# Gate halves ahead of the transposes in one branch, turned probabilities ahead of chunk splits in another

## The chip, the cores and the metric

The kernel runs on one core of one Trainium2 chip. The metric is the device time of one execution in microseconds; lower is better. TensorE is called PE here, VectorE DVE, ScalarE ACT, GpSimd POOL and SyncE SP, as in the profile.

## The reference, cut to what matters

Two layers of a streaming encoder run for 512 prompt frames and 8 running streams of 16 frames. Each layer mixes three attention branches and then applies a feed-forward part:

```python
h = _rms(x, p['norm_mix'])
(fq, fk, fv, fg, bq, bk, bv, iq, ik, iw, cqa, ckva, ckpe) = jnp.split(h @ p['w_in'], ...)
ya = fox attention(fq, fk, fv, decay)              # branch 1, "fox", 6 heads
yb = attention over the keys an indexer picks      # branch 3, "dsa", 4 heads
yc = latent attention with a rotary part           # branch 2, "mla", 6 heads
g = jax.nn.sigmoid((h @ p['w_gate']))              # gates: 1024 -> 3072
ga, gb, gc = jnp.split(g, 3, axis=-1)
x = x + (ga * ya @ ... + gb * yb @ ... + gc * yc @ ...) @ p['w_o']
x = x + SwiGLU(_rms(x))
```

The indexer of branch 3 scores all keys with 8 heads and keeps the best ones for each frame; 128 of them for the prompt.

## The kernel before, in words

**Items and steps.** The attention of a layer is cut into 88 items, in this order: 24 prompt items of the first branch (fox, one head and one tile of 128 queries each), 8 stream items of it (foxs, steps from `I_FOXS` = 24), 24 prompt items of the second branch (mla, steps from `I_MLA` = 32), 8 stream items (mlas, from `I_MLAS` = 56), 16 of the third branch (dsa, from 64) and 8 of its streams. A prompt item of query tile t has 128(t+1) keys, so its tiles are 128, 256, 384 or 512 columns wide; t goes 0, 0, 1, 1, 2, 2, 3, 3 over eight mla items. Every engine runs through the same steps, in its own order. An item goes through a softmax pipeline: PE computes `scores(i)` at step i, DVE the negated row maximum (`maxima`), ACT the exponential (`exp`), DVE the reciprocal of its sum, ACT multiplies by it at step i+1 (`normalise`), PE transposes the probabilities at step i+2 (`turn`), ACT copies them from PSUM (`turned_out`), and PE multiplies them with the values at step i+3 (`values`; for prompt items once for four items). The scores of item i use PSUM bank i % 3. The transposes use bank 3, or bank 7 where the side work leaves it free.

**Side work.** `SIDE[step]` lists other work of a step, sorted by `_ORDER`: indexer heads (`index_split`, `index_turn`, `index`, `index_sum`, steps 0 to 25), the rounds that pick the best keys (`pick`, DVE alone, one in each step from 0), the projections of the second branch (`mla_latent`, `mla_expand`, `mla_norm`, `mla_turn`, around steps 23 to 30), and the keys of its streams (`mlas_keys`, `mlas_norm`, around steps 53 to 61). On PE the first half of a step's list, by number of entries, comes ahead of `turn`, the second half behind `values`; on ACT the whole list comes ahead of `turned_out`.

**Gate halves.** The 48 gate halves are the products of h with `w_gate`: 24 matmuls of 320 columns each (three for each of 8 blocks, since every operand is split into a high and a low part), all into the one PSUM bank 5. PE computes half k in `gate_half(k)` in the step given by `GATE_AT`; it waits until ACT has copied half k-1 out of the bank (`g_moved`). ACT does that copy in `gate_move(k)` in the step after; behind the copy of an odd half it also makes the high part of a weight chunk (`hi`), and DVE the low part (`lo`), which frees the raw chunk for SP's next load. In the second branch's prompt items, the halves 21 to 29 are computed in steps 35, 37, ... 51, half 30 in step 52. In the first branch's prompt items there is one in every even step. `HELD` (half 17, step 22) is new in the change.

**ACT's order in a step** is: `normalise(step-1)`, `outputs(step-4)`, the gate moves of the step before, the side work, `turned_out(step-2)`, `outputs` of stream items, `exp(step)`. In steps that have an `index_turn` (the odd ones from 1 to 23) the gate moves come behind the side work, ahead of `turned_out`. Both are copies with the ACTIVATE instruction of line 1491, told apart by their output: `gst` or `g` is a gate half, `w_hi` a chunk's high part, `probs_t` the turned probabilities, `probs` the normalised ones. Line 945 is a gate half's matmul, 1121 a turn, 1141 the prompt values, 1062 and 1063 the scores of an mla item and their mask, 1205 the last products of `mla_expand`, 1607 the exponential, 1658 the indexer's copy.

Of the kernel before, what the change touches and what calls it, by code (L numbers as in the profile page):

```python
# [59 lines left out]
C_GATE = C_IN + 4 * len(GROUPS)  # L60
# [9 lines left out]
_c, _n = C_FF, C_FF  # L70
# [61 lines left out]
I_FOX, I_MLA, I_DSA = 0, len(FOX_ITEMS), len(FOX_ITEMS) + len(MLA_ITEMS)  # L132
ALL_ITEMS = FOX_ITEMS + MLA_ITEMS + DSA_ITEMS
N_ITEMS = len(ALL_ITEMS)
I_FOXS, I_MLAS, I_DSAS = I_MLA - DECB, I_DSA - DECB, N_ITEMS - DECB
# [9 lines left out]
SIDE = [[] for _ in range(N_ITEMS + 6)]  # L145
# [17 lines left out]
    SIDE[2 * _n].append(("index_split", _n))  # L163
    SIDE[2 * _n + 1].append(("index_turn", _n))
for _n in range(len(PICKS)):
    SIDE[_n].append(("pick", _n))
SIDE[I_DSA + 6].append(("mla_streams", 0))
SIDE[I_MLAS - 10].append(("mla_absorb", 0))
for _k in range(2):
    SIDE[I_MLAS - 13 + _k].append(("mla_rope", _k))  # L170
_ORDER = ("index_sum", "foxs_out", "mlas_out", "dsas_out", "mla_streams", "mla_turn", "mla_rope", "mla_absorb", "mla_norm", "mlas_norm", "mla_expand", "mlas_keys", "mla_latent",
          "foxs", "dsas_keys", "index", "index_turn", "index_split", "pick")
for _side in SIDE:
    _side.sort(key=lambda part: _ORDER.index(part[0]))
# [39 lines left out]
_total, _sum, GATE_AT = sum(GATE_WEIGHT[item[0]] for item in ALL_ITEMS), 0, [-1] * GATE_FIRST  # L214
# [4 lines left out]
                       else _n + (_n == I_MLAS - 3))  # L219
assert len(GATE_AT) == GATE_HALVES  # L220
GATE_KEPT = 6
GATE_LAST, LAST_PARTS = GATE_HALVES - 1, ((0, 3), (3, 6), (6, KD))
GATES_IN = [[_k for _k in range(GATE_HALVES) if GATE_AT[_k] == _n] for _n in range(N_ITEMS + 6)]

# [55 lines left out]
def build_program(nc, io):  # L280
    ctx = ExitStack()
    with ctx:
# [304 lines left out]
        def own_wait(eng, tick):  # L587

            eng.sem_inc(tick.sem, 1)
# [267 lines left out]
        def _(pe):  # L857
# [23 lines left out]
            for L in range(DEPTH):  # L881
# [109 lines left out]
                for c in range(2, C_GATE):  # L991
                    g, k = divmod(c, 4)
# [343 lines left out]
                for step in range(N_ITEMS + 6):  # L1336
                    if step < N_ITEMS:
                        scores(step)

                    half = (len(SIDE[step]) + 1) // 2  # L1340
                    for kind, n in SIDE[step][:half]:
                        beside(kind, n)
                    last_four = step in (I_FOXS + 2, I_MLAS + 2, I_DSAS + 2)
                    if last_four:
                        values(step - 3)
                    if 2 <= step < N_ITEMS + 2:
                        turn(step - 2)
                    if 3 <= step < N_ITEMS + 3 and not last_four:
                        values(step - 3)
                    for kind, n in SIDE[step][half:]:  # L1350
                        beside(kind, n)
                    for k in GATES_IN[step]:
                        if k != GATE_LAST:
                            gate_half(k)
                    if step in (N_ITEMS - 1, N_ITEMS, N_ITEMS + 1):
                        gate_half(GATE_LAST, *LAST_PARTS[step - N_ITEMS + 1])
                    if step == N_ITEMS + 2:
                        pe.wait_ge(it_exp.sem, it_exp.at(L, N_ITEMS))
                        own_wait(pe, pe_tick)
                        pe.wait_ge(lo_made.sem, lo_made.at(L, C_OUTS + 1))  # L1360
                        pe.wait_ge(at_lo.sem, at_lo.at(L, 1))
                        column_tile(0, C_OUTS, 0, 3, (h_hi[:, 0:3, :], h_lo[:, 0:3, :])).then_inc(y_done.sem, 1)
# [126 lines left out]
        def _(act):  # L1489
# [6 lines left out]
            for L in range(DEPTH):  # L1496
# [79 lines left out]
                def gate_move(k):  # L1576

                    m, half = divmod(k, 2)
                    if half:
                        act.wait_ge(w_used.sem, w_used.at(L, C_GATE + m + 1))  # L1580
                    else:
                        act.wait_ge(g_done.sem, g_done.at(L, m + 1))
                    if m >= 3 * GATE_KEPT:
                        dst = graw[m // 3][:, m % 3, half * HALF:(half + 1) * HALF]
                    else:
                        dst = gst[:, half, :]
                        if m:
                            act.wait_ge(g_out[half].sem, g_out[half].at(L, 16 * m))
                    copy(dst, ps[:, 5, 0:HALF]).then_inc(g_moved.sem, 1)
                    if half:  # L1590
                        if k != GATE_LAST:
                            hi(C_GATE + 2 + m, m % 2)

                def heads_out(dst, n, kd, t, h0, scale=1.0):
# [15 lines left out]
                def turned_out(i):  # L1610
                    _, _, _, rows, blocks, _ = item_shape(i)
                    act.wait_ge(it_tr.sem, it_tr.at(L, i + 1))
                    if PT_FREE[i]:
                        act.wait_ge(it_pv.sem, it_pv.at(L, PT_FREE[i]))
                    view = lambda a: a.rearrange("p (j r) -> p j r", r=P)[:, :, 0:rows]
                    copy(view(probs_t[:, PT_AT[i]:PT_END[i]]), view(ps[:, TURN_BANK[i], 0:blocks * P])).then_inc(it_pt.sem, 1)
# [159 lines left out]
                for step in range(N_ITEMS + 6):  # L1776
                    if step == 6:
                        act.wait_ge(store_dsa.sem, store_dsa.at(L, 3 * STORED))
                        act.wait_ge(store_fox.sem, store_fox.at(L, 3 * STORED))
                        act.wait_ge(store_mla.sem, store_mla.at(L, 2 * STORED))  # L1780
                    if 1 <= step <= N_ITEMS:
                        normalise(step - 1)
                    if 4 <= step < N_ITEMS + 4 and item_shape(step - 4)[3] == P:
                        outputs(step - 4)
                    moves = [k for k in GATES_IN[step - 1] if k != GATE_LAST] if step else []
                    turning = any(kind == "index_turn" for kind, n in SIDE[step])
                    if not turning:
                        for k in moves:
                            gate_move(k)
                    if step == N_ITEMS + 2:  # L1790
                        gate_move(GATE_LAST)
                    for kind, n in SIDE[step]:
                        beside(kind, n)
                    if turning:
                        for k in moves:
                            gate_move(k)
                    if 2 <= step < N_ITEMS + 2:
                        turned_out(step - 2)
                    if 3 <= step < N_ITEMS + 3 and item_shape(step - 3)[3] != P:
                        outputs(step - 3)  # L1800
                    if step < N_ITEMS:
                        exp(step)
# [201 lines left out]
        def _(dve):  # L2004
# [9 lines left out]
            for L in range(DEPTH):  # L2014
# [5 lines left out]
                def lo(c, slot, width=1024):  # L2020

                    dve.wait_ge(hi_made.sem, hi_made.at(L, c + 1))
                    high, low = split_of(c)
                    dve.tensor_tensor(low[:, 0:width], raw[raw_slot(c)][:, 0:width], high[:, 0:width].bitcast(F32), ALU.subtract).then_inc(lo_made.sem, 1)  # L2024
# [361 lines left out]
                def at_split(k0, nk, a):  # L2386
                    dve.wait_ge(rows_free.sem, rows_free.at(L, k0 // 3 + 1))
                    dve.wait_ge(tp_out.sem, tp_out.at(L, JOB["mla_streams", 0] + 1))
                    dve.tensor_copy(h_hi[:, k0:k0 + nk, :], a[:, :, :])
                    dve.drain()  # L2390
                    at_rest(k0, nk, a)
# [4 lines left out]
                for it in range(N_ITEMS + 6):  # L2396
                    if it == 0:
                        for k in range(1, GATE_FIRST // 2):
                            lo(C_GATE + 2 + k, k % 2)
                    if it == 6:  # L2400
                        dve.wait_ge(store_dsa.sem, store_dsa.at(L, 3 * STORED))
                        dve.wait_ge(store_fox.sem, store_fox.at(L, 3 * STORED))
                        dve.wait_ge(store_mla.sem, store_mla.at(L, 2 * STORED))
                    if 1 <= it <= N_ITEMS:
                        reciprocal(it - 1)
                    if it < N_ITEMS:
                        maxima(it)
                    if it == N_ITEMS:
                        at_split(0, 3, at_fox)
                    for kind, n in SIDE[it]:  # L2410
                        beside(kind, n)
                    for k in GATES_IN[it - 1] if it else ():
                        if k % 2 and k != GATE_LAST:
                            lo(C_GATE + 2 + k // 2, k // 2 % 2)
                at_split(3, 3, at_mla)
                dve.wait_ge(w_used.sem, w_used.at(L, C_OUTS))
                dve.wait_ge(it_out.sem, it_out.at(L, I_DSAS))
# [94 lines left out]
                for half in range(2):  # L2512
                    k, cols = slice(4 * half, 4 * half + 4), slice(P, T_COPIED * P)
# [211 lines left out]
```

## Time and profile before

| | |
|---|---|
| time, median of 3 runs | 2130.53 us (2129.0 to 2130.67) |
| profiled execution | 2130.57 us, span 2128.8 us |
| PE busy | 2092.0 us (98%) |
| DVE busy | 1394.2 us (65%) |
| ACT busy | 965.3 us (45%) |
| POOL busy | 395.8 us (19%) |
| DMA | 207.84 MB, 98 GB/s on the mean |

Times in the rows below are microseconds from the span's start; "idle before" is the time that the engine had nothing to run just ahead of the instruction, and the arrow names what it waited for. A layer takes about half the span. The steps of the first layer lie at 180 to 261 (fox), 261 to 317 (foxs), 317 to 400 (mla), the same steps of the second layer 1055.5 later.

### The profile page before, as it was taken

How to read it: one execution, taken by the hardware profiler on the slowest of the kernel's cores; microseconds unless marked ns; L12 is line 12 of the kernel's file. 1: busy time of each engine (PE TensorE's matmuls, PEld its weight loads, DVE VectorE, ACT ScalarE, POOL GpSimd, SP SyncE). 2: the span in 40 equal slices, each digit the busy share in tenths (PEclk: the TensorE clock that was granted, in tenths of full speed). 3: DMA queues.
4: the chain of work that ended last, by engine and by line, in shares of the span. 5: the costliest groups of instructions: out<-in, count | busy, mean ns of one | idle time of the engine just before them, and what ended most of it. 6: DMA issues, size and time to landing. Idle time of an engine off the chain costs nothing.

```text
span 2128.8 us, 36960 instructions
## 1 busy us (share of the span) xinstructions
PE 2092.0 (98%) x13616; PEld 1880.5 (88%) x13616; DVE 1394.2 (65%) x2839; ACT 965.3 (45%) x2054; POOL 395.8 (19%) x287
## 2 busy tenths in 40 slices
PE   9999999999999999999999999999999999999999
PEld 8998768788979989989899987787889899899897
DVE  4467876646749838839445778766476597496493
ACT  4246666566335314324232467665663343243241
POOL 1120030200004314224011200203000152241230
PEclk9999999999999999999999999999999999999999
DMA  6233224142422222222232332241424222222222
GB/s 219 76 113 124 72 93 134 56 141 88 139 79 80 88 82 80 86 76 87 78 138 77 111 115 89 80 138 56 150 85 139 80 80 87 73 85 85 80 90 79
DMA packets 90682, 207.84 MB, mean 98 GB/s; under 512 B 20676, under 2 KB 46920, under 8 KB 90184
## 3 DMA queue, kind: packets, MB, share of 16 engines
q1 hardware_dynamic: 90504, 205.48, 28.5%
q8 instruction: 110, 1.80, 0.3%
q14 instruction: 68, 0.56, 0.1%
HBM read 181.50 MB, written 23.95 MB: 97 GB/s over the span
## 4 chain that ended last, share of the span: by engine, by line
PE 91%; DVE 3%; ACT 3%; issue 1%; POOL 1%; DVEq 1%; DMA 0%; SPq 0%; ACTq 0%
PE ps L899 28%; PE ps L945 16%; PE ps L1430 8%; PE ps L1432 8%; PE ps L1431 8%; PE ps L957 7%; PE ps L1121 2%; PE ps L1141 2%; PE ps L1017 2%; PE ps L1062 1%; PE ps L1036 1%; PE ps L1235 1%; PE ps L1410 1%; POOL rsq L1969 1%; DVEq L2017 1%
## 5 line engine op out<-in xcount | busy, mean ns | idle before, releaser
L1491 ACT ACTIVATE w_hi<-raw 128x1024 fp32r<-128x1024 f32 (+4 forms) x172 | 171.2, 998 | 399.5 <-PE ps L899 369.3
L2024 DVE TENSOR_TENSOR w_lo<-raw,w_hi 128x1024 fp32r<-128x1024 f32 (+4 forms) x124 | 139.1, 1123 | 190.2 <-ACT w_hi L1491 186.2
L945 PE MATMUL ps<-h_hi,w_hi 128*128 128x320 f32 x768 | 246.1, 320 | 2.7 <-ACT g L1491 2.7
L945 PE MATMUL ps<-h_hi,w_lo 128*128 128x320 f32 x768 | 237.3, 309 | 0.0
L945 PE MATMUL ps<-h_lo,w_hi 128*128 128x320 f32 x768 | 237.2, 309 | 0.0
L1430 PE MATMUL ps<-th_hi,op_hi 128*128 128x320 f32 x640 | 198.3, 310 | 4.1 <-issue 4.1
L1969 POOL TENSOR_TENSOR rsq<-ssq,mhalf 128x12 f32<-128x12 f32 (+3 forms) x56 | 118.0, 2107 | 443.8 <-DVE ssq L2102 383.9
L1432 PE MATMUL ps<-th_hi,op_lo 128*128 128x320 f32 x640 | 198.5, 310 | 0.0
L1431 PE MATMUL ps<-th_lo,op_hi 128*128 128x320 f32 x640 | 198.2, 310 | 0.0
L899 PE MATMUL ps<-w_hi,act_hi 128*128 128x512 f32 x440 | 174.5, 396 | 0.0
L899 PE MATMUL ps<-w_hi,act_lo 128*128 128x512 f32 x440 | 174.4, 396 | 0.0
L899 PE MATMUL ps<-w_lo,act_hi 128*128 128x512 f32 x440 | 174.4, 396 | 0.0
L1491 ACT ACTIVATE op_hi<-w_sums 128x512 fp32r<-128x512 f32 x160 | 100.1, 631 | 143.5 <-PE ps L1432 117.1
L2485 DVE TENSOR_TENSOR w_lo<-raw,w_hi 128x1024 fp32r<-128x1024 f32 x48 | 59.9, 1252 | 157.9 <-ACT w_hi L1491 157.9
L945 PEld LDWEIGHTS ps<-h_hi,w_hi 128*128 128x128 f32 x768 | 144.3, 188 | 9.1 <-issue 5.9
L1431 PE MATMUL ps<-h_lo,op_hi 128*128 128x320 f32 x480 | 148.6, 310 | 0.0
L1430 PE MATMUL ps<-h_hi,op_hi 128*128 128x320 f32 x480 | 148.4, 309 | 0.0
L1432 PE MATMUL ps<-h_hi,op_lo 128*128 128x320 f32 x480 | 148.3, 309 | 0.0
L899 PE MATMUL ps<-w_hi,h_hi 128*128 128x384 f32 (+3 forms) x440 | 146.4, 333 | 0.4 <-DVE w_lo L2024 0.4
L899 PE MATMUL ps<-w_lo,h_hi 128*128 128x384 f32 (+3 forms) x440 | 146.2, 332 | 0.0
L899 PE MATMUL ps<-w_hi,h_lo 128*128 128x384 f32 (+3 forms) x440 | 145.9, 332 | 0.0
L1992 POOL TENSOR_TENSOR w_sums<-raw 128x512 f32<-128x512 f32 x40 | 63.7, 1593 | 438.3 <-DMA raw<-in_weights 215.7
(376 smaller groups left out, 5405.1 us busy)
## 6 DMA issues: line engine op xcount, KB each, us to landing
raw<-in_weights SPq DMA_DIRECT2D x212, 512.0 KB, 3.3
gates<-gst SPq DMA_DIRECT2D x72, 160.0 KB, 1.8
g<-gates SPq DMA_DIRECT2D x12, 960.0 KB, 6.8
raw<-in_weights SPq DMA_DIRECT2D x24, 384.0 KB, 3.0
ktb<-in_cache_fox_kt SPq DMA_DIRECT2D x16, 384.0 KB, 3.9
vc<-in_cache_fox_v SPq DMA_DIRECT2D x16, 384.0 KB, 3.8
x_sb<-in_x_prompt SPq DMA_DIRECT2D x8, 512.0 KB, 5.1
out_y_prompt<-x_sb SPq DMA_DIRECT2D x8, 512.0 KB, 3.3
```

The source lines that it names most:

```text
L899: mm = pe.matmul(ps[:, bank % 8, 0:width], x_pair[x][:, k0 + kk, t * P:(t + 1) * P], w[:, kk * width:(kk + 1) * width], start=first and kk ...
L945: mm = pe.matmul(ps[:, 5, 0:HALF], w[:, kk * P:(kk + 1) * P], h_pair[x][:, kk, half * HALF:(half + 1) * HALF], start=kk == 0 and n == 0, s ...
L957: mm = pe.matmul(ps[:, 2 * pair + half, 0:HALF], w[:, (w0 + kk) * P:(w0 + kk + 1) * P], x_pair[x][:, kk, half * HALF:(half + 1) * HALF], s ...
L1017: last = pe.transpose(ps[0:cols, bank, n * P:n * P + rows], src, cst("ident", 0, rows, rows))
L1430: pe.matmul(ps[:, bank, 0:HALF], op_hi[i][:, a], x_hi, start=first and kk == 0, stop=False, skip_group_check=not first)
L1431: pe.matmul(ps[:, bank, 0:HALF], op_hi[i][:, a], x_lo, start=False, stop=False, skip_group_check=not first)
L1432: mm = pe.matmul(ps[:, bank, 0:HALF], op_lo[i][:, a], x_hi, start=False, stop=kk == 3, skip_group_check=not first)
L1491: return act.activation(dst, src, ACT.Copy, scale=scale)
L1969: pool.tensor_tensor(rsq[:, n % RSLOT, 0:width], ssq[:, n % RSLOT, 0:width], mhalf[:, 0:width], ALU.pow).then_inc(sq_root.sem, 1)
L1992: pool.tensor_tensor(w_sums[:, 0, :], up_first(c), up_second(c), ALU.add).then_inc(sums_made.sem, 1)
L2024: dve.tensor_tensor(low[:, 0:width], raw[raw_slot(c)][:, 0:width], high[:, 0:width].bitcast(F32), ALU.subtract).then_inc(lo_made.sem, 1)
L2485: dve.tensor_tensor(w_lo[c % 2][:, :], raw[raw_slot(c)][:, :], w_hi[c % 2][:, :].bitcast(F32), ALU.subtract).then_inc(lo_made.sem, 1)
```

## The change

It has four parts.

1. `leading`: in steps 34 to 51 PE computes a gate half between the first half of the side work and `turn(step-2)`, not at the end of the step. ACT's and DVE's orders do not change for it.
2. In ACT's steps with an `index_turn`, `turned_out(step-2)` comes ahead of the gate moves (and of the `hi` in them).
3. `HELD`: the `hi` and `lo` of the chunk that came behind gate half 17 (step 23) move to the end of step 24, on ACT behind `turned_out(22)`.
4. `pick` rounds from number 24 on come two steps later (none in steps 24 and 25, the last in step 58, not 56), and `index_sum` comes behind `mla_norm` (which alters step 25). As PE's half of a step is counted by entries, `mla_expand` 1 moves from before `turn` to behind `values` in step 25, and `mlas_keys` 4 and 5 move from the end of steps 57 and 58 to before `turn` and `values`.

```diff
 for _n in range(len(PICKS)):
-    SIDE[_n].append(("pick", _n))
+    SIDE[_n + 2 * (_n >= I_FOXS)].append(("pick", _n))
...
-_ORDER = ("index_sum", "foxs_out", "mlas_out", "dsas_out", "mla_streams", "mla_turn", "mla_rope", "mla_absorb", "mla_norm", "mlas_norm", "mla_expand", "mlas_keys", "mla_latent",
+_ORDER = ("foxs_out", "mlas_out", "dsas_out", "mla_streams", "mla_turn", "mla_rope", "mla_absorb", "mla_norm", "mlas_norm", "index_sum", "mla_expand", "mlas_keys", "mla_latent",
...
+HELD = GATE_AT.index(I_FOXS - 2)
+assert HELD % 2 and GATE_AT[HELD + 1] >= I_FOXS + 2
...
+                    leading = I_MLA + 2 <= step < I_MLAS - 4
+                    for k in GATES_IN[step] if leading else ():
+                        gate_half(k)
                     if 2 <= step < N_ITEMS + 2:
                         turn(step - 2)
                     if 3 <= step < N_ITEMS + 3 and not last_four:
                         values(step - 3)
                     for kind, n in SIDE[step][half:]:
                         beside(kind, n)
-                    for k in GATES_IN[step]:
+                    for k in () if leading else GATES_IN[step]:
                         if k != GATE_LAST:
                             gate_half(k)
...
-                        if k != GATE_LAST:
+                        if k not in (HELD, GATE_LAST):
                             hi(C_GATE + 2 + m, m % 2)
...
+                    if 2 <= step < N_ITEMS + 2:
+                        turned_out(step - 2)
                     if turning:
                         for k in moves:
                             gate_move(k)
-                    if 2 <= step < N_ITEMS + 2:
-                        turned_out(step - 2)
+                    if step == GATE_AT[HELD] + 2:
+                        hi(C_GATE + 2 + HELD // 2, HELD // 2 % 2)
...
                     for k in GATES_IN[it - 1] if it else ():
-                        if k % 2 and k != GATE_LAST:
+                        if k % 2 and k not in (HELD, GATE_LAST):
                             lo(C_GATE + 2 + k // 2, k // 2 % 2)
+                    if it == GATE_AT[HELD] + 2:
+                        lo(C_GATE + 2 + HELD // 2, HELD // 2 % 2)
```

## Rows read from the trace of the kernel before

**Rows 1.** Page, part 4: the chain that ended last, by engine.

```profile
PE 91%; DVE 3%; ACT 3%; issue 1%; POOL 1%; DVEq 1%; DMA 0%; SPq 0%; ACTq 0%
```

**Rows 2.** Windows: stretch and length, busy of each engine, clock, DMA share, GB/s.

```profile
179.00:261.00 82.00, 78.91 (x582) 66.20 (x581) 68.53 (x185) 55.98 (x148) 0.58 (x1) 1.00 0.31 104
...
317.00:384.00 67.00, 67.00 (x544) 59.16 (x538) 42.85 (x121) 43.86 (x122) 2.80 (x4) 1.00 0.42 127
```

**Rows 3.** Waits of PE, 179 to 425: total, times, longest.

```profile
PE ps L1121 <- ACT probs_t L1491: 2.5, 4, 1.0
PE ps L1205 <- ACT sq_a L1669: 1.3, 1, 1.3
PE ps L1017 <- DVE qa L2123: 1.2, 1, 1.2
...
PE ps L1187 <- issue: 0.5, 2, 0.3
...
PE ps L1171 <- ACT at_mla L1491: 0.4, 1, 0.4
```

**Rows 4.** Timeline, steps 7 and 8: start, duration, engine, instruction.

```profile
204.33 0.42 ACT L1491 ACTIVATE gst<-ps 128x320 f32<-128x320 f32 x1
...
204.65 1.05 ACT L1491 ACTIVATE w_hi<-raw 128x1024 fp32r<-128x1024 f32 x1
...
205.59 0.48 ACT L1491 ACTIVATE probs_t<-ps 128x384 f32<-128x384 f32 x1
...
206.22 0.63 PE L1121 MATMUL ps<-consts,probs 128*128 128x128 f32 x4 [0.94 <-ACT probs_t L1491]
```

**Rows 5.** Timeline, step 25: the last index_sum pair on DVE.

```profile
272.33 1.04 DVE L2298 SCALAR_TENSOR_TENSOR pen<-relu,p_i,pen 128x256 f32<-128x256 f32 x2
```

**Rows 6.** Timeline, ACT in steps 39 and 40: 384 columns turned, 512 in the exponential.

```profile
339.89 0.48 ACT L1491 ACTIVATE probs_t<-ps 128x384 f32<-128x384 f32 x1
...
340.26 0.69 ACT L1607 ACTIVATE probs<-ps,mx 128x512 f32<-128x512 f32 x1
...
340.83 0.21 ACT L1607 ACTIVATION_READ_ACCUMULATOR probs<-ps,mx 128x1 f32 x1
...
341.27 0.73 ACT L1491 ACTIVATE probs<-probs,mx 128x512 f32<-128x512 f32 x1 [0.23 <-DVE mx L2276]
```

**Rows 7.** Timeline, PE in steps 40 and 41: scores, turn, (scores,) turn; ACT's copy.

```profile
342.78 0.38 PE L1062 MATMUL ps<-kt,qt 96*128 96x128 f32 x2
...
343.06 0.60 PE L1121 MATMUL ps<-consts,probs 128*128 128x128 f32 x4
...
343.79 0.60 PE L1121 MATMUL ps<-consts,probs 128*128 128x128 f32 x4
...
344.26 0.59 ACT L1491 ACTIVATE probs_t<-ps 128x512 f32<-128x512 f32 x1
```

**Rows 8.** Timeline, ACT in steps 42 to 44: the same chain on narrow tiles.

```profile
348.66 0.27 ACT L1491 ACTIVATE probs_t<-ps 128x128 f32<-128x128 f32 x1
...
348.90 0.47 ACT L1607 ACTIVATE probs<-ps,mx 128x256 f32<-128x256 f32 x1
...
349.27 0.19 ACT L1607 ACTIVATION_READ_ACCUMULATOR probs<-ps,mx 128x1 f32 x1
...
350.03 0.51 ACT L1491 ACTIVATE probs<-probs,mx 128x256 f32<-128x256 f32 x1 [0.56 <-DVE mx L2276]
```

**Rows 9.** Timeline, step 52: scores (384 columns), turn, first matmul of gate half 30.

```profile
379.37 0.81 PE L1062 MATMUL ps<-kt,qt 96*128 96x384 f32 x2
...
380.07 0.39 PE L1121 MATMUL ps<-consts,probs 128*128 128x128 f32 x2
...
380.22 0.39 PE L945 MATMUL ps<-h_hi,w_hi 128*128 128x320 f32 x1
```

**Rows 10.** Timeline, second layer, third branch: a gate half that waits for the copy.

```profile
1505.32 0.44 ACT L1491 ACTIVATE g<-ps 128x320 f32<-128x320 f32 x1 [0.88 <-PE ps L945]
...
1505.90 0.38 PE L945 MATMUL ps<-h_hi,w_hi 128*128 128x320 f32 x1 [0.51 <-ACT g L1491]
```

## The prediction

> **What bounds the kernel now.** I read the chain that ended last first: 91% of it is PE [rows 1], and PE is busy for 98% of the span (the table above). So a change of order can only win what PE waits, and it loses whatever new wait it puts on PE. The busy share of PE has to be read with care, since the ends of matmuls are modelled; so I also took the distances between starts of neighbouring instructions, which are what PE's time is made of. Next come the windows of the stages [rows 2]. In the first branch's prompt steps PE is busy for 78.91 of 82 us, so about 3 us a layer are open there. In the second branch's prompt steps it is busy for 67.00 of 67.00: PE waits for nothing in the very stretch where part 1 of the change works. The waits of PE over both [rows 3] name what ends them: the turned probabilities (2.5 us in 4 waits, the copy that frees the transposes' bank), the squares of `mla_expand` (1.3, step 24), the heads of `mla_norm` (1.2, step 26), the indexer's score matmul (0.5 in 2, which the profile calls issue; by the program it also waits for a turned copy, in bank 7), and the copies around steps 58 and 59 (0.4). The second layer has the same waits 1055.5 us later. The sum is made for one layer and doubled.
>
> **Part 2, turned copies first in indexer steps.** The pattern is in [rows 4]: ACT copies the gate half (204.33), splits the chunk (204.65, 1.05 us long), and only then copies the turned probabilities (205.59 to 206.07); PE starts its next transposes 0.15 us later, at 206.22, after 0.94 us of idleness. In the new order that copy starts at about 204.33, ends at 204.81, and PE could start at 204.96; the wait is gone. All four waits for turned copies lie behind an odd gate half and so behind a split, so 2.5 us a layer are within reach, and 0.5 more at the two indexer matmuls, 3.0 in all. I don't take all of it. ACT does the same work in the step in all, so `exp` starts no earlier than before, and the split ends 0.4 us later, with DVE's low part, the reciprocal and the normalisation behind it. PE is about 1 us earlier at the next step, where the transposes share bank 7 with the indexer's copies: I take 0.3 us back for each of the two large waits, and nothing for the two indexer matmuls, because their copy waits for transposes that come just before. 2.5 - 0.6 = 1.9 us a layer. Bounds: 1.2 (half of the four given back downstream) and 3.0. What hides the moved split: the chunk is used several steps later, and no wait of PE for a chunk is among [rows 3]. SP's store of the gate half and its next chunk load are issued 0.4 us later, with the same cover.
>
> **Parts 3 and 4, steps 23 to 26.** Without the split in step 23 (1.05 us, the length in [rows 4]) ACT reaches the squares of `mla_expand` 0 about 1 us earlier, which is most of the 1.3 us wait. The split now lies behind the turned copy of step 24, where ACT had gaps while PE computes; DVE's low part takes the place of the pick that left step 24. In step 25 `mla_norm` 0 no longer stands behind the index sums, 1.04 us [rows 5], nor behind a pick; the low part (a bit over 1 us) comes in ahead of it. That takes the 1.2 us wait at step 26 as well, except that PE also arrives 1 us earlier. Of 1.3 + 1.2 = 2.5 I take 2.1; bounds 0.9 (only one of the two goes) and 2.5. SP: the load of the chunk that follows waits for the held low part, and two key loads stand behind it in SP's queue, now some 5 us later; their scores are in steps 28 and 29, over 20 us on, so that costs nothing. The picks end at step 58, ten steps before their result is used.
>
> **Part 4, steps 57 to 59.** `mlas_keys` 4 on PE now stands ahead of the transposes, as on ACT; the turned copy is no longer late for the values of step 58 and for the transposes of step 59, and so neither are the values of the stream item (0.4 in [rows 3], and about as much in two waits of 0.2 to 0.3). I take 0.7, bounds 0.2 and 1.0. The two added picks lie in DVE time that waits for POOL's roots. The gains together: 1.9 + 2.1 + 0.7 = 4.7 us a layer, bounds 2.3 and 6.5.
>
> **Part 1, leading gate halves.** Nothing can be won in a stretch without a wait [rows 2]. What it costs is a new wait. `turn(n-2)` now stands behind gate half k on PE. On ACT `turned_out(n-2)` waits for it, and behind it in the same queue stand `exp(n)`, whose scores have been ready for 3.6 us, then `normalise(n)`, then `gate_move(k)`; and the next gate half on PE waits for that move. Before, all but the move itself ran during the gate half. I count from the start of `turn(n-2)`, for n = 39:
>
> - ACT: the turn of three blocks ends after 0.49 (0.60 for four blocks less one, [rows 7]), the copy starts 0.03 later and `exp` 0.37 behind it; `exp` with its accumulator read takes 340.26 to 341.04, 0.78; the normalisation starts 0.23 later and holds ACT for 0.63 of its 0.73 [rows 6]. The gate copy starts at 2.53, takes 0.44, and PE starts 0.14 behind its end, as 1505.76 to 1505.90 [rows 10]: 3.11 us.
> - PE: turn of three blocks 0.35, then scores, turn, scores of steps 40 and 41, 342.78 to 343.79 = 1.01 [rows 7]: 1.36 us. It waits 3.11 - 1.36 = 1.7 us (1.75).
>
> The same for the others, with the short tiles of [rows 8] (copy to `exp` 0.24, `exp` 0.56, gap 0.23, normalisation 0.42) and 0.70 for scores of 384 columns [rows 9]:
>
> - n = 35, 43: ACT 0.31 + 0.24 + 0.56 + 0.23 + 0.42 + 0.44 + 0.14 = 2.34; PE 0.1 + 0.70 + 0.22 + 0.70 = 1.72; wait 0.6.
> - n = 37, 45: two scores of 512 columns and values of 12 matmuls lie between, over 3.2 us; wait 0.
> - n = 41, 49: 28 value matmuls lie between, so the gate half doesn't wait; but the values do, for the copy of their last item's four blocks: 0.60 + 0.03 + 0.59 + 0.15 = 1.37 [rows 7] against 0.44 + 0.5 + 0.2 of PE; wait 0.2.
> - n = 51: half 30 comes already in step 52, behind one item. 379.37 to 380.22 is 0.85 [rows 9], with the turn 0.95; wait 2.34 - 0.95 = 1.4.
>
> Sum: 2(0.6 + 0 + 1.75 + 0.2) + 1.4 = 6.5 us a layer. Bounds: 5.0 (0.15 less for each, where ACT pipelines its instructions more closely, and no wait of the values) and 7.3 (0.1 more at each seam). Such a wait occurs in this kernel already: where two gate halves lie close together in the third branch, the half waits 0.51 us for the copy [rows 10]. ACT and DVE have time to catch up in the next gate half (3.6 us against about 3), so waits don't add up over pairs.
>
> A rule of the Trainium skill speaks against this part: PSUM — Partial Sum Buffer, section Engine vs sequencer instructions, calls ScalarE's queue strict FIFO. The trace agrees: in [rows 4] the copy of transposes that were long done starts only behind the split. By that rule the sum stands as it is; without it the 6.5 would be nearly nothing.
>
> **Sum.** 2 x (6.5 - 4.7) = +3.6 us. The profiled execution took 2130.57 us (span 2128.8 and 1.8 around it), 0.04 over the median, so both give 2134.1 us, +0.17%.
>
> **Rivals.**
> - A, gains and cost cancel: ACT's chain is a little shorter than I count (5.0) and parts 2 to 4 win 5: 2130.5. For it: the waits of [rows 3] are real and the chain has nine links, each read to 0.05.
> - B, the other side, faster: the late exponential doesn't reach the gate copy. The wait arises only if the way from the turn to the copy's end is longer than PE's stretch between two gate halves; it decides from about 1.3 us on (n = 51 and 39), and I count 2.3 to 3.1. If it were shorter, only 0.4 us a layer would be lost and the result would be 2130.5 - 2 x 4.3 = 2122. Against it: [rows 6], where exponential and normalisation alone take 1.6 us.
> - C, parts 2 to 4 win only their lower bound, because ACT's and DVE's chains take back what PE gains, and part 1 costs 7.3: 2130.5 + 2 x (7.3 - 2.3) = 2140.5. For it: in steps 0 to 23 ACT and DVE are busy for 56 and 69 of 82 us [rows 2].
> - D, the new idle stretches lower PE's granted clock. Against it: it is 1.00, the 2.4 GHz level, in the window that has the waits of 0.9 and 1.0 us [rows 2]. A gate half of 3.6 us at half the clock costs 3.6 more, 18 of them 65 us: 2199.
>
> The Trainium skill, TensorE: Matmul & The Clock Gate, section A second HAM failure mode, tells of short, frequent idleness of PE lowering its clock; this is D, and no row here shows it.
>
> **Chances.** My forecast (2131.5 to 2137) 0.54; A 0.20; C 0.14; B 0.08; D 0.02; something else 0.02. No change within 0.2% (2126.3 to 2134.8) is about what a measurement of this kernel can tell. The forecast's case lies across its upper edge, 0.34 below and 0.20 above. Same 0.34 + 0.20 = 0.54; slower 0.20 + 0.14 + 0.02 + 0.01 = 0.37; faster 0.08 + 0.01 = 0.09. Range 2129.5 to 2138.5: it takes in A and most of the way to C; B, D and the end of C are left out.
>
> **What would show it.** Right: PE with new waits for ACT `gst` at line 945 between 340 and 400, largest ahead of halves 24, 28 and 30 (1.4 to 1.8 us); the waits for `probs_t` between 180 and 260 gone but for some tenths; no 1.2 us wait for `qa` at step 26. PE reaches step 32 about 4 us earlier, step 53 about 2.5 later. Wrong: PE still without a wait in the second branch's prompt steps (B), or waits that shift to other instructions of the first branch, normalised rows or the indexer's bank (C).

## The result: 4.16 us slower, and the profile after

The changed kernel takes 2133.93 us (median of 20 runs, 2131.72 to 2135.56); the kernel before took 2129.77 us in the same session (20 runs, 2128.33 to 2131.49). The ratio is 1.002, 95% interval 1.0013 to 1.0027. The prediction was 2134.1 us. The profiled execution took 2133.68 us, with a span of 2131.9.

PE is still busy for 98% of the span. Its share hides two gains (first branch, steps 57 to 59) and a loss (second branch). Part 4 of the page, the chain that ended last, by engine; it answers to [rows 1]:

```profile
PE 89%; DVE 4%; ACT 4%; issue 2%; DVEq 1%; POOL 1%; DMA 0%; ACTq 0%; SPq 0%
```

The windows of the same two stretches, as [rows 2]:

```profile
179.00:261.00 82.00, 81.33 (x605) 68.41 (x603) 70.78 (x192) 57.52 (x154) 0.58 (x1) 1.00 0.32 106
...
317.00:384.00 67.00, 61.98 (x464) 53.95 (x463) 38.62 (x106) 39.39 (x109) 3.80 (x4) 1.00 0.37 113
```

In the first branch PE's busy time rose from 78.91 to 81.33 us of 82; in the second it fell from 67.00 to 61.98. The waits of PE from 179 to 425 (total, times, longest), as [rows 3]; the line numbers are 2 higher on PE, 5 on ACT and 7 on DVE:

```profile
PE ps L947 <- ACT gst L1496: 4.9, 5, 1.6
PE ps L1019 <- ACT qt L1496: 0.9, 3, 0.5
PE ps L1207 <- ACT sq_a L1674: 0.8, 1, 0.8
PE ps L1189 <- ACT probs_t L1496: 0.5, 2, 0.3
```

The 2.5 us for turned probabilities and the 1.2 for `qa` are gone, the squares went from 1.3 to 0.8, and a wait of 4.9 us in 5 pieces is new: gate halves, for ACT's copy of the half before. The 0.5 at the indexer's score matmuls stays. Part 2 at work, in the timeline of steps 7 and 8 (start, duration, engine, instruction), as [rows 4]:

```profile
203.94 0.48 ACT L1496 ACTIVATE probs_t<-ps 128x384 f32<-128x384 f32 x1
...
204.31 0.44 ACT L1496 ACTIVATE gst<-ps 128x320 f32<-128x320 f32 x1
...
204.63 1.06 ACT L1496 ACTIVATE w_hi<-raw 128x1024 fp32r<-128x1024 f32 x1
204.74 0.60 PE L1123 MATMUL ps<-consts,probs 128*128 128x128 f32 x4
```

The turned copy comes first, and PE's next transposes start at 204.74 without a wait. Part 1 at work, in the timeline of steps 39 to 41; its ACT rows answer to [rows 6]:

```profile
338.67 0.49 PE L1123 MATMUL ps<-consts,probs 128*128 128x128 f32 x3
...
339.19 0.50 ACT L1496 ACTIVATE probs_t<-ps 128x384 f32<-128x384 f32 x1 [2.69 <-PE ps L1123]
...
339.58 0.68 ACT L1612 ACTIVATE probs<-ps,mx 128x512 f32<-128x512 f32 x1
...
340.15 0.20 ACT L1612 ACTIVATION_READ_ACCUMULATOR probs<-ps,mx 128x1 f32 x1
340.38 0.16 DVE L2283 RECIPROCAL mx<-mx 128x1 f32<-128x1 f32 x1 [3.16 <-ACT probs L1612]
...
340.58 0.72 ACT L1496 ACTIVATE probs<-probs,mx 128x512 f32<-128x512 f32 x1 [0.23 <-DVE mx L2283]
...
341.21 0.42 ACT L1496 ACTIVATE gst<-ps 128x320 f32<-128x320 f32 x1
...
341.77 0.38 PE L947 MATMUL ps<-h_hi,w_hi 128*128 128x320 f32 x1 [1.61 <-ACT gst L1496]
```

This is the chain of the prediction. ACT is idle for 2.69 us during the gate half, because the first thing in its queue, the turned copy, needs a turn that PE now does behind the gate half. Exponential, reciprocal and normalisation follow one by one, and the gate copy behind them starts 2.54 us after the turn. The way from the turn to the next gate half is 341.77 - 338.67 = 3.10 us (counted: 3.11).

The busy columns can't be subtracted to price this, since they are taken over fixed times in which the two kernels do different work; distances between PE's starts can. I read three stretches in each layer: from the indexer's sums for the streams, just ahead of step 0, to the scores of step 32; from there to the first work on the streams' latents in step 53; and from there to the first product with the output weights. A cell with two values is first layer / second layer. The starts of the middle stretch in the first layer, before and changed:

```profile
317.43 0.49 PE L1062 MATMUL ps<-kt,qt 96*128 96x128 f32 x2
...
384.52 0.86 PE L1235 MATMUL ps<-wkv,ctb 128*128 128x384 f32 x2
```

```profile
313.09 0.49 PE L1064 MATMUL ps<-kt,qt 96*128 96x128 f32 x2
...
386.68 0.86 PE L1237 MATMUL ps<-wkv,ctb 128*128 128x384 f32 x2
```

| kernel | steps 0 to 32 | 32 to 53 | 53 to the end |
|---|---|---|---|
| before | 153.75 / 153.75 | 67.09 | 133.13 |
| changed | 149.53 / 149.83 | 73.59 | 132.31 |
| difference | -4.22 / -3.92 | +6.50 | -0.82 |

A layer is 1.5 to 1.8 us longer, two are 3.2; predicted were 3.6. The rest of the measured 4.16 is in the last section. Such a distance has noise of its own: the changed kernel and those of experiments 1, 5, 6, 8 and 10 are alike up to step 32, and in the first layer five of them take 149.50 to 149.55 us to there, but that of experiment 1 150.38.

### The profile page after: what moved, and what is told of

The parts are those of the page before. It is cut to its first block, busy times and chain, and to the rows that moved or that the text cites. A ratio compares the mean times of both kernels' runs of the same rounds, so it can differ in the third digit from the quotient of the medians.

```text
span 2131.9 us, 36960 instructions
## 1 busy us (share of the span) xinstructions
PE 2093.9 (98%) x13616; PEld 1881.2 (88%) x13616; DVE 1392.4 (65%) x2839; ACT 963.4 (45%) x2054; POOL 397.0 (19%) x287
## 4 chain that ended last, share of the span: by engine, by line
PE 89%; DVE 4%; ACT 4%; issue 2%; DVEq 1%; POOL 1%; DMA 0%; ACTq 0%; SPq 0%
PE ps L901 28%; PE ps L947 15%; PE ps L1435 8%; PE ps L1436 8%; PE ps L1437 8%; PE ps L959 7%; PE ps L1123 2%; PE ps L1143 2%; PE ps L1019 2%; PE ps L1237 1%; PE ps L1038 1%; PE ps L1064 1%; PE ps L1415 1%; PE ps L1202 1%; POOL rsq L1976 1%
```

## The experiments

All were timed against the kernel before, in three sessions: its medians were 2130.56 (kernels 1 to 4), 2130.37 (5 to 8) and 2129.52 (9 and 10). Its runs fall into levels by their mean granted clock: medians of 2128.96 at 1.000 (24 runs), 2130.58 at 0.999 (27) and 2132.05 at 0.998 (4). Within a level the runs still lie up to 1.7 and 2.4 us apart; the medians at 0.999 of the three sessions are 2130.69, 2130.52 and 2130.64. Where medians mix these levels, I compare runs at 0.999; the changed kernel's median there is 2133.84 (13 of its 20 runs).

**1. Without part 1.** `leading` is always false.

```diff
-                    leading = I_MLA + 2 <= step < I_MLAS - 4
+                    leading = False
```

> Everything of the change but part 1 (the gate halves of the second branch's prompt items stay at the end of the step). Theory (ACT's late chain: the turned copy, exponential and normalisation stand between the turn and the gate copy, and only the gate halves and values of steps 34 to 53 pay for it, 6.5 us a layer by the distances of PE's starts in the two traces): 2133.9 - 13.0 = 2120.9, against the kernel before -4.2 to step 32 and -0.8 around step 58, twice, -10.1 us, so 2119.7 to 2121. Rival 1 (part of PE's time at these steps comes from elsewhere, for example from where the stretch at half clock falls): only the gate waits themselves go, 4.9 us a layer, 2124. Rival 2 (what parts 2 to 4 win is given back later if PE does not lose it in the second branch): 2125 to 2130.

Measured: 2120.87 us (5 runs), ratio 0.9956 (0.9943 to 0.9968); 2120.84 at 0.999. Steps 32 to 53 take 67.10 us, as before. So part 1 alone turns a kernel that would be 9.7 us faster into one that is 3.3 slower. Both rivals fall: the cost is more than the 4.9 us a layer of recorded waits, and nothing of the gains is given back later (the last stretch takes 132.31, as in the changed kernel).

**2. Part 1 alone,** on the kernel before: the two edits of PE's loop, nothing else.

> Part 1 alone, on the kernel before. Theory: the cost does not depend on the other parts, since it is made within each pair of steps: +13.0 us against the kernel before, 2142.8, with waits of gate halves of 0.26, 1.61, 0.34, 1.61 and 1.05 us in steps 35 to 52 as in the changed kernel. Rival (the earlier PE of parts 2 to 4 meets ACT and DVE less far ahead, so part of the cost is theirs): clearly less, +9 to +11.

Measured: 2143.49 us (5 runs, all at 0.999), ratio 1.006 (1.0046 to 1.0074), +12.9. The waits of PE between 300 and 425 in this kernel:

```profile
PE ps L945 <- ACT gst L1494: 4.9, 5, 1.6
...
PE ps L1141 <- ACT probs_t L1494: 0.2, 1, 0.2
```

Steps 32 to 53 take 73.58 us. The cost is the same with and without the other parts, so it is made inside the pairs of steps, and the rival of a shared cost falls.

**3. Part 2 alone,** on the kernel before.

```diff
+                    if 2 <= step < N_ITEMS + 2:
+                        turned_out(step - 2)
                     if turning:
                         for k in moves:
                             gate_move(k)
-                    if 2 <= step < N_ITEMS + 2:
-                        turned_out(step - 2)
```

> Part 2 alone, on the kernel before: the turned copy ahead of the gate copy and chunk split in indexer steps. Theory by the prediction's term: 1.9 us a layer, -3.8 us, 2126.0; the four waits of the transposes gone. PE is by the trace of the changed kernel 2.5 us earlier at step 23; rival: without parts 3 and 4 the squares and heads of steps 24 and 26, which are set by ACT and DVE, take nearly all of it back (their waits grow from 1.3 and 1.2): less than 1 us a layer, -1 to -2 us, 2128 to 2129.

Measured: 2126.22 us (11 runs), ratio 0.9979 (0.9970 to 0.9988); 2126.15 at 0.999, -4.4. Steps 0 to 32 take 151.36 / 151.68 us, 2.39 / 2.07 less. The waits of PE from 179 to 425:

```profile
PE ps L1205 <- ACT sq_a L1669: 1.9, 1, 1.9
PE ps L1017 <- DVE qa L2123: 1.2, 1, 1.2
```

The four waits for turned copies are gone. The wait for the squares has grown from 1.3 to 1.9: 0.6 us a layer is given back, the size that the prediction took off, but at step 24 and not at the steps behind the large waits. The wait for `qa` did not grow. The rival, that these two waits take nearly all of it back, falls.

**4. Parts 3 and 4 alone.** The changed kernel with `leading` false and the order of part 2 undone.

> Parts 3 and 4 together, without parts 1 and 2, on the kernel before. Theory by the prediction's terms: 2.1 + 0.7 us a layer, -5.6 us, 2124.2. If the parts are additive, this and part 2 alone make the whole of the kernel without part 1, -10. Rival (steps 23 to 26 can only give what PE had not already waited for the turned copies): the two waits shrink as in the changed kernel and give 2.0 to 2.4 there, 0.8 at step 58, -6.4 us, 2123.4, and part 2 alone is then worth more in company than alone.

Measured: 2124.2 us (7 runs), ratio 0.9972 (0.9961 to 0.9983). Four of the seven runs have a mean clock of 1.000, with a median of 2123.92: 5.0 less than the kernel before at 1.000. The trace says the same: steps 0 to 32 take 151.98 in both layers (1.77 less), the last stretch 132.30 (0.83 less), together 5.2. Waits of PE from 179 to 425:

```profile
PE ps L1123 <- ACT probs_t L1496: 2.5, 4, 1.0
...
PE ps L1207 <- ACT sq_a L1674: 0.3, 1, 0.3
```

Experiments 3 and 4 together make 2.23 + 1.77 = 4.0 us a layer up to step 32; the changed kernel has 4.2 / 3.9. The parts are additive within the noise of such a distance. The rival had the same form with a price of -6.4. That the median of 2124.2 is 6.4 below the session's, and is just the 2124.2 expected, comes from its mix of clocks; at equal clock the parts win 5.0 to 5.2, less than the 5.6 expected.

**5. Exponential and gate copy first.** The changed kernel, with part 1 kept on PE, and ACT's order fitted to it in steps 35, 37, ... 51.

```diff
-                    moves = [k for k in GATES_IN[step - 1] if k != GATE_LAST] if step else []
+                    leads = lambda n: I_MLA + 2 <= n < I_MLAS - 4
+                    moves = [k for k in GATES_IN[step - 1] if k != GATE_LAST and not leads(step - 1)] if step else []
...
+                    early = leads(step) and GATES_IN[step]
+                    if early:
+                        exp(step)
+                        for k in GATES_IN[step]:
+                            gate_move(k)
                     if 2 <= step < N_ITEMS + 2:
                         turned_out(step - 2)
...
-                    if step < N_ITEMS:
+                    if step < N_ITEMS and not early:
                         exp(step)
```

> The changed kernel, with ACT's order fitted to part 1: in the steps with a leading gate half ACT does the exponential of the step, then the copy of that gate half, and only then the turned copy. The gate copy no longer stands behind anything that needs the turn. Theory (ACT's order is the whole cost of part 1): the waits of the gate halves vanish; the values of steps 41 and 49 wait 0.2 to 0.4 us for the turned copy, so 2120.9 + 0.8 to 1.6 = 2121.7 to 2122.5. Rival 1 (a gate half ahead of the transposes costs PE by itself, by the bank or by its neighbours in the array): stays near 2133.9. Rival 2 (the turned copy, now 0.5 us later, makes the transposes of the next item wait in their place): 2126 to 2130.

Measured: 2122.24 us (5 runs), ratio 0.9966 (0.9953 to 0.9978); 2121.99 at 0.999, 11.9 less than the changed kernel, with PE's order the same instruction by instruction. ACT around step 39:

```profile
338.48 0.44 ACT L1496 ACTIVATE gst<-ps 128x320 f32<-128x320 f32 x1 [2.04 <-PE ps L947]
338.81 1.05 ACT L1496 ACTIVATE w_hi<-raw 128x1024 fp32r<-128x1024 f32 x1
...
339.76 0.49 ACT L1496 ACTIVATE probs_t<-ps 128x384 f32<-128x384 f32 x1
340.13 0.72 ACT L1496 ACTIVATE probs<-probs,mx 128x512 f32<-128x512 f32 x1
```

The gate copy now follows its gate half at once, and no gate half waits from 300 to 425. Nor do transposes wait in their place (rival 2). ACT's order was nearly the whole cost. Left are 0.66 us (67.75 us from step 32 to 53) in both layers, and that is the most that a gate half ahead of the transposes costs PE by itself (rival 1). By the starts of scores, 0.15 of it comes in each of steps 42 and 50, where the prompt values need the turned copy, and the other 0.36 in pieces of up to 0.05 in the steps between. The chunk split stands ahead of the turned copy here, which starts 1.48 us behind the turn (338.28); an order without this lateness was not tried.

**6. Exponential first,** gate copy left in the step after.

> The changed kernel, with ACT's exponential ahead of the turned copy in the steps with a leading gate half; the gate copy stays in the step after. Theory: the exponential (0.78 and a gap of 0.15 to 0.23) leaves the chain from the turn to the gate copy. Left by the prediction's sums: steps 35 and 43 nothing, 39 and 47 2.1 - 1.36 = 0.75, 41 and 49 0.2, step 51 0.6, so 2.5 us a layer in place of 6.5: 2120.9 + 5.0 = 2125.9. Rival (the chain is not what sets the wait, the copy of the gate half itself or DVE's part is): 2132 to 2134.

Measured: 2126.02 us (11 runs), ratio 0.9982 (0.9973 to 0.9991); 2126.09 at 0.999, against 2125.9 expected. The waits of PE from 300 to 425:

```profile
PE ps L947 <- ACT gst L1496: 1.5, 3, 0.6
```

Three waits stay, as the sums had it, and the two of steps 35 and 43 are gone. Steps 32 to 53 take 69.80 us, 2.7 a layer over the 67.1 (counted: 2.5). The rival (2132 to 2134) falls. The largest went from 1.61 to 0.60, about the length of the exponential with its accumulator read and the gap behind it. The chain is what sets them.

**7. Part 4 without the held split.** As experiment 4, with gate half 17's split back in step 23.

```diff
-HELD = GATE_AT.index(I_FOXS - 2)
-assert HELD % 2 and GATE_AT[HELD + 1] >= I_FOXS + 2
+HELD = -1
...
-                    if step == GATE_AT[HELD] + 2:
-                        hi(C_GATE + 2 + HELD // 2, HELD // 2 % 2)
...
-                    if it == GATE_AT[HELD] + 2:
-                        lo(C_GATE + 2 + HELD // 2, HELD // 2 % 2)
```

> Part 4 alone on the kernel before: the picks two steps later and index_sum behind mla_norm; gate half 17's chunk split stays in step 23. Parts 3 and 4 together took 6.4 us off. Theory: the 1.2 us wait of step 26 and about 0.8 around step 58 go, the 1.3 us wait of step 24 stays: 2 x 2.0, -4.0 us, 2126.5; the held split is worth the other 2.4. Rival (at step 24 the split on ACT is not what makes PE wait; the heads of step 26 and the picks are all of it): -6, 2124.2.

Measured: 2127.14 us (11 runs), ratio 0.9988 (0.9979 to 0.9997); 2127.09 at 0.999, -3.5. Waits of PE from 179 to 425:

```profile
PE ps L1122 <- ACT probs_t L1495: 2.8, 5, 1.0
PE ps L1206 <- ACT sq_a L1673: 1.3, 1, 1.3
```

The wait for `qa` is gone and that for the squares is as before; in experiment 4, without the split there, it is 0.3. So the split on ACT is what made the squares late, and the rival falls. Up to step 32 the new order wins 0.66 / 0.61 us, the held split the other 1.1 of the 1.77. Half of the 1.2 us of the `qa` wait is taken back; one more wait for a turned copy is among what takes it.

**8. Only every second gate half leading.**

```diff
-                    leading = I_MLA + 2 <= step < I_MLAS - 4
+                    leading = step in (I_MLA + 3, I_MLA + 7, I_MLA + 11, I_MLA + 15)
```

> The changed kernel, with only every second gate half of the stretch ahead of the turn (steps 35, 39, 43, 47); those of 37, 41, 45, 49 and 51 at the end of their step. Between a leading half and the next one there are then two whole steps of PE's work with both turns, between the others the exponential has run in time. Theory (the wait is ACT's chain of 2.3 to 3.1 us less PE's stretch between two leading halves, 1.0 to 1.7 us): the next stretch is longer than the chain, so next to nothing is left: 2121 to 2122. Rival (each leading half has a cost of its own): four ninths of 13.0, 2126.7.

Measured: 2129.2 us (11 runs), ratio 0.9994 (0.9985 to 1.0003); 2127.97 at 0.999. Both miss: at 0.999 it is 6 to 7 us over mine and 1.3 over the rival's 2126.7. Steps 32 to 53 take 70.68 us, 3.6 a layer over the 67.1. No gate half waits, but another instruction does. The timeline around step 41:

```profile
338.38 0.49 PE L1123 MATMUL ps<-consts,probs 128*128 128x128 f32 x3
...
339.30 0.68 ACT L1612 ACTIVATE probs<-ps,mx 128x512 f32<-128x512 f32 x1
...
340.30 0.72 ACT L1496 ACTIVATE probs<-probs,mx 128x512 f32<-128x512 f32 x1 [0.23 <-DVE mx L2283]
...
341.07 0.66 PE L1123 MATMUL ps<-consts,probs 128*128 128x128 f32 x4 [1.19 <-ACT probs L1496]
```

It is the same late exponential with another customer. Item 39's normalised rows are ready 2.64 us after the start of the turn of step 39, and PE comes to their transposes in step 41 after two short steps. In the changed kernel a gate half stands ahead of those transposes and meets the chain first. I had asked only who waits for the gate copy.

**9. All splits last.** Experiment 1, and in all indexer steps the split goes behind the exponential too (`gate_move(k, False)` is a gate copy without its split).

```diff
                     if turning:
                         for k in moves:
-                            gate_move(k)
+                            gate_move(k, False)
...
                         exp(step)
+                    if turning:
+                        for k in moves:
+                            if k % 2 and k != HELD:
+                                hi(C_GATE + 2 + k // 2, k // 2 % 2)
```

> The change without part 1, and in all indexer steps the chunk split also goes behind the exponential on ACT (as part 3 does for one of them). Left in the kernel without part 1 are 0.8 us for the squares at step 24, 0.5 for the indexer's copy in bank 7, 0.4 for a turned copy, and 0.5 at the indexer matmuls, a layer. Theory: the exponential and the work behind it come 1.05 us earlier in six steps; the 0.5 and the 0.4 go in part: 2120.9 - 0.5 to 1.5 = 2119.4 to 2120.4. Rival (ACT does the same work in all, and the later split makes DVE's low part and the next chunk late): 2121 to 2123.

Measured: 2122.57 us (6 runs), ratio 0.9969 (0.9957 to 0.9980); 2124.79 in its one run at 0.999, where experiment 1 has 2120.84, and 2122.4 in four at 1.000. So it is slower than experiment 1. One run prices that poorly; by the starts, steps 0 to 32 take 151.31 / 151.49 us, 1.8 / 1.7 more than the changed kernel's same steps, 3.4 in all (2.6 against experiment 1, whose first layer is the long one). The waits of PE from 179 to 425:

```profile
PE ps L1123 <- ACT relu L1663: 1.3, 2, 0.7
PE ps L1207 <- ACT sq_a L1674: 1.1, 1, 1.1
```

The split now stands ahead of the next step's normalisation and indexer copy, and the transposes that share bank 7 wait for that copy, up to 0.71 us. The rival was right in size; what came late is the indexer's copy, not a chunk. Holding one split back where ACT has a gap pays (experiment 7); holding all back moves the wait.

**10. Every second gate half leading, exponential first.** Experiment 8 with `exp(step)` ahead of `turned_out(step-2)` in its four steps.

> As the kernel with every second gate half leading, with the exponential ahead of ACT's turned copy in those four steps. There the turn of step 41 (and 49) waited 1.19 us for the normalised probabilities of item 39: the late exponential, whose next customer is the turn when no gate half stands ahead of it. Theory (one chain, turned copy to exponential to normalisation, and whoever reads its result first pays): with the exponential out of the chain that wait goes and 2121 to 2122 is left, 6 to 7 us less than the 2128 of that kernel at the same mean clock. Rival (a leading gate half costs about 0.8 us each by itself): stays at 2127 to 2129.

Measured: 2122.59 us (6 runs), ratio 0.9966 (0.9954 to 0.9979); 2122.47 at 0.999, 5.5 less than experiment 8 there. The waits of its transposes for normalised rows:

```profile
PE ps L1123 <- ACT probs L1496: 0.4, 2, 0.2
```

From 1.2 to 0.2 us each. Steps 32 to 53 take 68.03 us, 0.94 a layer over the 67.1, so the time stays half a microsecond above the 2121 to 2122 expected. The late exponential was most of the cost in experiment 8; the rival of a fixed 0.8 us for each leading half falls.

Experiment 1 is the best version: 2120.87 us, 13 less than the changed kernel and 9.7 less than the one before.

## Why the prediction was right, step by step

- **Part 2** (1.9 us a layer): 2.1 to 2.4 alone. The waits went as read, and the 0.6 given back was seen, at the squares. The 0.2 to 0.5 beyond 1.9 is in no recorded wait.
- **Parts 3 and 4, steps 23 to 26** (2.1): 1.77 alone. The two waits were 2.5; the squares still wait 0.3 there, and 0.8 in company, since PE comes earlier. With part 2, 4.0 predicted and 4.2 / 3.9 measured up to step 32. The two misses have opposite signs and nearly cancel; that is luck.
- **Part 4, steps 57 to 59** (0.7): 0.82.
- **Part 1** (6.5): 6.50. By the starts of scores in the first layer: from step 34 to 38 0.50 (counted 0.6), to 42 1.89 (1.95 with the values), to 46 0.75 (0.6), to 50 1.89 (1.95), to 53 1.47 (1.4). In the first layer PE is 4.2 us earlier at step 32 (about 4 said) and 2.3 later at step 53 (about 2.5 said). The recorded waits are only 4.9: the one ahead of half 30 is 1.05, under the 1.4 to 1.8 of the forecast's signs, and the values' 0.2 is among no row (0.15 by the starts of step 42). Of the 1.6 us between 4.9 and 6.5, 0.66 is in experiment 5 too, which has PE's order and no gate wait; the other 0.97 is about 0.2 for each of the five waits. Part of that is how a wait is counted, from the modelled end of the matmul before it: in step 41 PE had 341.77 - 1.61 - 338.67 = 1.49 us of work by that, where the starts gave 1.36. The rest is not explained. Adding recorded waits would have put the cost 1.6 us a layer too low. The stated lower bound of 5.0 doesn't follow from its reasons: 0.15 off each of five waits and no wait of the values make 6.5 - 0.75 - 0.4 = 5.35.
- **The time.** That 2133.93 stands within 0.2 us of the 2134.1 is in part luck too. The forecast starts from 2130.5, the time of the profiled execution at a mean clock of 0.999; at that clock the change costs 3.3 us and not 3.6. The +4.16 is larger because the kernel before, by its times, ran about half of the result's session without a fall of the clock (last section).
- **Rivals.** A had 5.0 for part 1: it is 6.5, though the total is near. B is refuted by the changed kernel and experiment 2, where the late exponential does reach the gate copy. C's lower bounds did not occur. D did not occur: the granted clock is 1.00, the 2.4 GHz level, in the window that has the new waits of up to 1.61 us. The rule of the Trainium skill (PSUM — Partial Sum Buffer, section Engine vs sequencer instructions) that ScalarE's queue is strict FIFO agrees with these traces: in step 39 of the changed kernel ACT is idle for 2.69 us ahead of the turned copy, though the scores of the exponential behind it began at 334.07, and experiments 5 and 6, which alter nothing but ACT's order, take 11.9 and 7.8 us off, at a clock of 0.999.
- **Too simple** was my picture of who pays. I named the gate half as the customer of the late exponential; experiment 8 shows a second, the transposes of its normalised rows.

## What to carry to other kernels

Before an instruction block is moved ahead of another on one engine, list what the other engines have queued behind their next wait for the block that was overtaken. Here moving 3.6 us of matmuls ahead of 0.4 us of transposes held back an exponential whose input had long been ready, and it cost 13 us; with ACT's order changed too (experiment 5), 1.3 us of that was left by the starts. Take the path from the late producer to each of its customers, not only to the nearest, and compare it with what the consumer has to do in between. In a stretch where the bounding engine waits for nothing, leave its order alone.

## What the runs showed of the hardware

Much of the scatter of these runs is TensorE's clock. In the feed-forward part of each layer PE once waits about 2 us, and behind that wait the granted clock falls to half, the 1.2 GHz level, for some microseconds, or it doesn't. In the kernel of experiment 5, first layer (PE's first instruction behind the wait, then windows; the clock is the third number from the right):

```profile
672.17 0.39 PE L1435 MATMUL ps<-th_hi,op_hi 128*128 128x320 f32 x1 [1.89 <-issue]
...
670.00:672.00 2.00, 0.28 (x2) 0.02 (x1) 1.91 (x4) 0.96 (x2) 0.00 (x0) 1.00 0.00 0
672.00:674.00 2.00, 1.83 (x10) 1.86 (x11) 1.91 (x5) 0.00 (x0) 0.00 (x0) 0.80 0.00 0
674.00:676.00 2.00, 2.00 (x10) 2.00 (x9) 1.49 (x4) 0.63 (x1) 1.81 (x2) 0.50 0.25 53
```

In the kernel of experiment 4, at the same place:

```profile
674.14 0.39 PE L1435 MATMUL ps<-th_hi,op_hi 128*128 128x320 f32 x1 [1.92 <-issue]
...
672.00:674.00 2.00, 0.21 (x2) 0.00 (x0) 1.91 (x4) 0.96 (x2) 0.00 (x0) 1.00 0.00 0
674.00:676.00 2.00, 1.86 (x13) 1.90 (x14) 1.91 (x5) 0.00 (x0) 0.01 (x1) 1.00 0.00 0
```

The wait is 1.89 us in the first and 1.92 in the second, and experiment 6 has 1.89 us without a fall, so its length alone does not decide. The kernel before shows both in one trace: its clock falls behind the wait of 1.91 us at 676 (0.50 from 678 to 680) and stays up behind that of 2.23 us at 1732 (1.00 from 1732 to 1738). A fall goes with 1.5 to 1.6 us: the kernel before takes 2128.96, 2130.58 and 2132.05 us at mean clocks of 1.000, 0.999 and 0.998, and in the twelve traces these three levels go with no, one and two such places (none in experiments 4, 6 and 9; two in experiments 5 and 7; one in the seven others). This accounts for the rest of the result. At 0.999 the change costs 2133.84 - 2130.58 = 3.3 us, the 3.2 of the starts; but 19 of the changed kernel's 20 runs had a mean clock under 1.000, and only 31 of the kernel before's 55 in the other sessions. In the result's own session the clocks of the kernel before are not on record; 11 of its 20 runs took 2128.33 to 2129.78 us, about the range of its level of 1.000 (2128.36 to 2130.09). Why a kernel falls more often was not tried. At this size of effect a difference of medians that mix clock levels can be off by up to 1.6 us: experiment 4's is 6.4 us, where equal clocks give 5.0.
